# Projection stage of a hybrid decoder layer: new places for the weight sums, the row loads and the last group order, and outputs stored from ScalarE's queue

## The reference

```python
h = rms_norm(x, g_mix)                 # 2048 x 1024
proj = h @ w_in                        # 1024 x 7168, columns in 14 blocks of 512:
# q, k, v of three attention groups (9), the S5 input u (1), gate_a and gate_b (4)
q = head_rms_norm(q, q_gain) * HEAD_DIM ** -0.5     # norm over each head's 64
k = head_rms_norm(k, k_gain)
# gates: sigmoid(gate_a), sigmoid(gate_b)
```

## Time and profile before

| | us |
|---|---|
| three runs, median (lowest, highest) | 4801.2 (4799.83, 4801.86) |
| the profiled execution | 4802.6 |
| its span, first to last instruction | 4801.0 |
| its mean granted clock | 0.978 of full |

### The profile page before, as it was taken

How to read it: one execution, slowest core, us unless ns; L and a number is a source line. 1 busy time by engine, 2 the same in 40 slices (tenths; PEclk the granted TensorE clock), 3 DMA queues, 4 the chain that set the end, 5 groups by cost and what they waited for, 6 DMA issues and landing times.

```text
span 4801.0 us, 76663 instructions
## 1 busy us (share of the span) xinstructions
PE 4579.8 (95%) x25756; PEld 4000.1 (83%) x25756; DVE 3153.2 (66%) x6216; ACT 2181.2 (45%) x3608; POOL 928.7 (19%) x911
## 2 busy tenths in 40 slices
PE   7989899999889999999799999999999999999998
PEld 6767688777679987788699999999988888999997
DVE  6646674666456678555555556666667777778887
ACT  4444353444336673133233334344445555556665
POOL 1433200244212101222111111111121111111121
PEclk9999999999999999999899999999999999999999
DMA  6887665555654445543445555656566566677777
GB/s 205 278 301 239 235 202 169 156 164 176 185 191 141 135 164 183 186 135 135 169 159 172 189 182 189 206 179 216 180 222 222 208 232 242 236 245 269 279 262 256
DMA packets 341070, 971.18 MB, mean 202 GB/s; under 512 B 46057, under 2 KB 77588, under 8 KB 303317
## 3 DMA queue, kind: packets, MB, share of 16 engines
q1 hardware_dynamic: 307704, 862.90, 51.2%
q0 software_dynamic: 28304, 88.03, 7.9%
q10 hardware_dynamic: 4829, 17.31, 1.0%
HBM read 772.82 MB, written 200.58 MB: 203 GB/s over the span
## 4 chain that ended last, share of the span: by engine, by line
PE 50%; DVE 1%; ACT 0%; issue 0%; DVEq 0%; POOL 0%; DMA 0%; ACTq 0%; SPq 0%; POOLq 0%
PE ex_d L2794 14%; PE ex_g L2761 11%; PE ex_g L2763 9%; PE ex_g L2757 7%; PE ex_d L2757 4%; PE ex_d L2788 3%; PE ex_d L2763 2%; PE ex_g L2738 1%; PE ex_d L2738 0%; DVE ex_x L2956 0%; PE ex_d L2769 0%; DVEq L2565 0%; ACT ex_wgh L2841 0%; DVE ex_y L3030 0%; ACT ex_x L2854 0%
## 5 line engine op out<-in xcount | busy, mean ns | idle before, releaser
L2763 PE MATMUL ex_g<-ex_x,ex_wgl 128*128 128x256 f32 (+12 forms) x3456 | 981.1, 284 | 0.0
L2761 PE MATMUL ex_g<-ex_x,ex_wgh 128*128 128x288 f32 (+5 forms) x3584 | 757.7, 303 | 3.7 <-DVE ex_x L2956 3.7
L2763 PEld LDWEIGHTS ex_g<-ex_x,ex_wgl 128*128 128x128 f32 x3456 | 653.0, 189 | 3.9
L2938 DVE TENSOR_TENSOR ex_wgl<-ex_wg,ex_wgh 128x2048 fp32r<-128x2048 f32 x274 | 626.6, 2287 | 41.4 <-ACT ex_wgh L2841 41.3
L2841 ACT ACTIVATE ex_wgh<-ex_wg 128x2048 fp32r<-128x2048 f32 x274 | 523.8, 1912 | 284.0 <-PE ex_g L2763 275.7
L2761 PEld LDWEIGHTS ex_g<-ex_x,ex_wgh 128*128 128x128 f32 x3584 | 594.2, 188 | 12.8 <-DVE ex_x L2956 3.9
L2757 PE MATMUL ex_g<-ex_x,ex_wgh 128*128 128x512 f32 (+6 forms) x1664 | 529.5, 376 | 1.0 <-DVE ex_t L2968 1.0
L878 DVE TENSOR_TENSOR prj_wl<-prj_raw,prj_wh 128x512 fp32r<-128x512 f32 x396 | 314.5, 806 | 294.0 <-ACT prj_wh L756 293.3
L703 PE MATMUL prj_p<-prj_wh,prj_ah 128*128 128x512 f32 x1136 | 459.1, 404 | 44.9 <-DVE prj_wl L878 42.8
L703 PE MATMUL prj_p<-prj_wh,prj_al 128*128 128x512 f32 x1136 | 450.4, 396 | 0.0
L703 PE MATMUL prj_p<-prj_wl,prj_ah 128*128 128x512 f32 x1136 | 450.0, 396 | 0.0
(11 more groups left out here) (449 smaller groups left out, 9391.4 us busy)
## 6 DMA issues: line engine op xcount, KB each, us to landing
ex_wg<-in_w_gu SPq DMA_DIRECT2D x276, 1024.0 KB, 5.1
ex_wd<-in_w_down SPq DMA_DIRECT2D x276, 512.0 KB, 5.7
prj_raw<-sums_d SPq DMA_DIRECT2D x208, 256.0 KB, 3.1
prj_raw<-in_w_in SPq DMA_DIRECT2D x188, 256.0 KB, 3.0
qkv_d<-prj_o SPq DMA_DIRECT2D x144, 256.0 KB, 3.4
wo_spare<-qkv_d SPq DMA_DIRECT2D x40, 768.0 KB, 4.3
prj_wt<-in_w_in SPq DMA_DIRECT2D x56, 512.0 KB, 5.4
sums_d<-prj_wt SPq DMA_DIRECT2D x28, 1024.0 KB, 5.1
```

Source lines behind the costliest of these rows:

```text
L2761: pe.matmul(out[:, 0:size], h[:, k, j, :], x[:, k, 0:size], start=(k == 0 and x is xh), stop=False)
L2763: last = pe.matmul(out[:, 0:size], l[:, k, j, :], xh[:, k, 0:size], start=False, stop=(k == KD - 1))
L2938: tt(flat(wgl[z][:, :, :, :]), flat(wg[r][:, :, :, :]), flat(wgh[z][:, :, :, :]).bitcast(F32), ALU.subtract).then_inc(wgl_ready, 1)
```

## The change

The weight sums of pairs 1 to 6 are placed seven steps apart from step 4 on (before, all 28 in 5.78 steps each from step 8 on); those of pair 0 run at steps 226 to 247, and wait until the row blocks have left `wt`. Half 1 takes its pairs in the order 1, 4, 5, 0, 6, 2, 3 (before 0, 1, 4, 5, 6, 2, 3). Row tiles are loaded at `LOAD_AT` and normalised at `NORM_AT`, ahead of `TILE_AT`. `store` moves from SP to ScalarE, to the end of its step, behind the splits. The padding transfers are issued one every seven steps from 94 on, and VectorE makes three small groups a step in place of five.

```diff
-    for half, order in ((0, (0, 1, 2, 3, 4, 5, 6)), (1, (0, 1, 4, 5, 6, 2, 3))):
+    for half, order in ((0, (0, 1, 2, 3, 4, 5, 6)), (1, (1, 4, 5, 0, 6, 2, 3))):
...
+    LOAD_AT = {1: 3, 2: 4, 3: 5, 5: 6, 10: 7}
+    NORM_AT = {1: 2, 2: 3, 6: 4, 7: 5, 9: 6, 13: 7}
     TILE_AT = {1: 2, 2: 3, 9: 4, 11: 5, 13: 6, 15: 7}
     PAIR_AT = (42, 53, 64, 75)
-    SUM_AT = [8 + 156 * k // 27 for k in range(NQ * KH)]
+    LATER = KH * (NQ - 1)
+    SUM_AT = [4 + 7 * k for k in range(LATER)] + [226 + 7 * k for k in range(KH)]
...
+    PADS_AT = range(ZERO + 6, TABLES, 7)
...
-                        if half == 0:
+                        if half == 0 or q == 0:
                             sp.wait_ge(sum_out, 16 * SUMS.index((q, kk)) + 16)
...
-                    if k:
+                    if k == LATER:
+                        sp.wait_ge(turned, NB1)
+                    elif k:
                         sp.wait_ge(sum_out, 16 * k)
...
-                    if g == ZERO + 4:
-                        sp.wait_ge(zeroed, 1)
-                        for dst in pads:
-                            sp.dma_start(dst, xt[2][:, :]).then_inc(pads_out, 16)
+                    if g in PADS_AT[:len(pads)]:
+                        if g == PADS_AT[0]:
+                            sp.wait_ge(zeroed, 1)
+                        sp.dma_start(pads[PADS_AT.index(g)], xt[2][:, :]).then_inc(pads_out, 16)
+                    if g == PADS_AT[len(pads)]:
                         for dst, src in fills:
...
+                def store(e):
+                    g, kind, (_, where), half, upper, j = outs[e]
+                    if kind == Q:
+                        act.wait_ge(q_done, q_no[e] + 1)
+                    elif e in g_no:
+                        act.wait_ge(gated, g_no[e] + 1)
...
+                    act.dma_start(dst, ot[e % OR][:, :]).then_inc(o_out[e % OR], 16)
+
+                def store_at(e):
+                    g, kind = outs[e][:2]
+                    return g + (4 if kind == Q else 3 if e in g_no else 2)
...
-                for g in range(NSTEP + 3):
+                left = list(range(len(outs)))
+                for g in range(NSTEP + 4):
+                    if g in NORM_AT:
+                        square(NORM_AT[g])
+                        root(NORM_AT[g])
                     if g in TILE_AT:
                         b = TILE_AT[g]
-                        square(b)
-                        root(b)
                         high(2 * b)
                         high(2 * b + 1)
...
                         for s in splits_at(g):
                             split(s)
+                    while left and store_at(left[0]) <= g:
+                        store(left.pop(0))
...
+                    if g in NORM_AT:
+                        mean(NORM_AT[g])
+                        normalise(NORM_AT[g])
...
                     if MAPS <= g < TABLES:
-                        some(making_maps, 5)
+                        some(making_maps, 3)
```

More of the change, by code:

```diff
@@ L503, in load_block @@
                         sp.wait_ge(comb_out, stored[NJ])
-                        sp.wait_ge(sum_out, 16 * len(SUMS))
+                        sp.wait_ge(sum_out, 16 * LATER)
                     elif i >= NB0 + 4:
@@ L507, in load_block @@
                     sp.dma_start(dst, comb_d[j, o]).then_inc(sem, 16)
[L509 to L531, removed]
                 def load_maps():
@@ L575, in _ @@
                 loaded = KH + 1
-                left = list(range(len(outs)))
                 for g in range(NSTEP):
[L578 to L581, removed]
+                    if g in LOAD_AT:
+                        load_x(LOAD_AT[g])
                     ahead = min(NS, (g // NJ + 1) * KH + RAW + (0, 0, 1, 2)[g % NJ])
@@ L623, in _ @@
                 sp.wait_ge(pads_out, 16 * (len(pads) + len(fills)))
-                for e in left:
-                    store(e)
                 for z in range(2):
@@ L794, in head_squares @@
                         act.activation(sq[:, :], ot[e % OR][:, :], ACT.Square).then_inc(sq_ready, 1)
+                def store(e):
[4 more added lines that the diff above has]
+                        act.wait_ge(gated, g_no[e] + 1)
+                    elif g in act_post:
+                        act.wait_ge(act_done, act_post[g])
+                    else:
+                        act.wait_ge(dve_done, dve_post[g])
+                    t = 2 * NJ * half + NJ * upper + j
+                    if kind == GATE:
+                        c = 2 * half + upper
+                        dst = gate_d[:, where * NJ + j, c * CH:(c + 1) * CH]
+                    elif where is None:
+                        dst = u_d[t * P:(t + 1) * P, :]
+                    else:
+                        dst = qkv_d[where[0], t * P:(t + 1) * P, where[1], :]
+                    act.dma_start(dst, ot[e % OR][:, :]).then_inc(o_out[e % OR], 16)
+                def store_at(e):
+                    g, kind = outs[e][:2]
+                    return g + (4 if kind == Q else 3 if e in g_no else 2)
                 def head_roots(g):
@@ L1138, in _ @@
                 for g in range(NSTEP + 3):
+                    if g in NORM_AT:
+                        mean(NORM_AT[g])
+                        normalise(NORM_AT[g])
                     if g in TILE_AT:
                         b = TILE_AT[g]
-                        mean(b)
-                        normalise(b)
                         low(2 * b)
```

## The result

The changed kernel takes 4742.5 us (median of four runs, 4737.0 to 4743.5), the kernel before 4800.5 beside it (4793.0 to 4801.9): a ratio of 0.988, 95% interval 0.9863 to 0.9897. That is 58 us less, against 67 forecast (4734, range 4706 to 4768). The profiled execution took 4742.1 with a span of 4740.4; the projection's last matmul ends at 1213.9 us in place of 1274.7, 60.8 earlier, and the profiled executions differ by 60.5, so all of it came from the projection.

What follows compares the result with a forecast made beforehand. TensorE bounds the kernel, stalled in the projection by late weight slices queued behind SP's waits at sums. Gains 41 + 17 + 8 + 1 + 0 = 67 us gave 4734 us, range 4706 to 4768.

Steps and rivals of the forecast that it cites:

- The sum cycle: Weight sums' load, subtractions and store: 18.2 us with issues, too long for 15.7 us, just fitting seven steps, 19.0 us.
- Steps 32 to 115: Projection stretch with 58.5 us excess: queue waits go, DMA share 0.92 leaves 17; gain 41, bounds 36 and 58.
- Steps 116 to 171: Two q/k groups, excess 31.5 us: the stores' move decides, 14 kept; gain 17, bounds 3 and 22.
- The landing L: Time a q/k output store takes to land after ScalarE's issue; stores set VectorE's write period only from 6.1 us.
- Fewer small vector operations a step: VectorE's small groups in the projection's steps: gain 0, bounds 0 and 2 us.
- ScalarE's issues: 224 store issues of 0.34 us on ScalarE during the projection, delaying next to nothing: taken as 0.
- Rows ahead: First 17 steps: earlier row tile loads and norms remove PE's waits for tiles; gain 8 us, bounds 3 and 9.
- Half 1: Last four sums at steps 226 to 247 and the new pair order: gain 1 us, bounds -6 and +8.
- slower: Rival: ScalarE's late-landing stores close a loop with VectorE's writes in q/k groups; plus 43 us, 4844; chance 0.05.
- nothing: Rival: DMA sets the projection's pace, so fewer SP waits only move bytes; about 4797 us; chance 0.04.
- the waits only change place: Rival: sums' latency grows as DMA fills, SP stands again, q/k writes wait on stores; 4768 us; chance 0.16.
- all stalls go: Rival: all first-half stalls vanish, as DMA can run full and store landings are short; 4706 us; chance 0.13.

## Why the prediction was right, step by step
- *The sum cycle.* Right. 15.7 us didn't hold it: in the kernel before the loads of sums were 19.2 us apart in the mean of 22 gaps, with the dense sums put back 18.4, near the 18.2 that the prediction added up; and in the three kernels with dense sums steps 32 to 87 keep 29.1 to 30.6 us, in those with seven steps 15.6 to 23.3. The loads are now 20.7 us apart in the mean (58.1 at the second, 514.4 at the last of 22 gaps), not 19, which is seven steps at the pace that these steps had. It fits less well than the prediction had it: SP still waits 73 us at both lines, 30.8 of them at the first, where under 20 was said.
- *Steps 32 to 115: 41 forecast, 40.4 measured (287.8 to 247.4), the reason for the rest wrong.* That 17 us would stay, since DMA would be full at 0.92, came out in size alone, by luck: the stretch moved 73.1 MB, not 76.5, the share stayed at 0.85, and 11 MB more raised the stretch by 6 us. A share near 0.84 with PE still stalled was the prediction's own sign of being wrong; it was met, and it was this step that was wrong. What keeps the rest is open: 14.6 of the 18.5 us stand in products' first steps, behind VectorE's low halves, and most of the others in steps 37 and 38, where VectorE's write of an output is late.
- *Steps 116 to 171: 17 forecast, 16.7 measured, but not by its path.* The prediction said that the move of the stores decides here. Either change alone takes the excess: sums alone leave 5.4, stores alone 12.1, of 32.0. The full change keeps 15.4, of which 11.8 stand in steps 116 to 143; the next point has a likely reason. The landing L, where the danger was seen, is 3.6 us in these steps (median of the stores), within the 3 to 4 named beside the sum and far from 6.1; the loop doesn't close, though the 21 us named with it didn't come either. VectorE's writes in one group answer to the earlier trace rows, at 4.3 us a write:
```profile
516.02 0.69 DVE L895 TENSOR_TENSOR prj_o<-prj_p,prj_ua 128x512 f32<-128x512 f32 x1
...
519.83 0.69 DVE L895 TENSOR_TENSOR prj_o<-prj_p,prj_ua 128x512 f32<-128x512 f32 x1 [0.88 <-DMA qkv_d<-prj_o]
...
529.02 0.69 DVE L895 TENSOR_TENSOR prj_o<-prj_p,prj_ua 128x512 f32<-128x512 f32 x1
```
Of the four writes (another is at 523.93) only the second waited for a landing, 0.88 us where 5.16 had stood.
- *Fewer small vector operations a step: 0 forecast, never run alone.* Three groups a step in place of five last to step 124, where five end in step 112. In the first line below, the changed kernel, where step 116 begins at 368.5 us, some 20 us of this work fall in the first q/k group, in which VectorE is busiest; in the second, sums and order alone, all of it ends before that group (from 395.6):
```profile
L960 DVE TENSOR_SCALAR prj_x<-prj_x x10: 165/167/169, 376.6 to 398.0; 128x16 f32<-128x16 f32 x10
```
```profile
L957 DVE TENSOR_SCALAR prj_x<-prj_x x10: 160/167/169, 371.4 to 387.2; 128x16 f32<-128x16 f32 x10
```
All kernels with three groups have 7.4 to 13.4 us of excess in steps 116 to 143, sums and order alone has 1.5. Neither the stores, the row loads nor the padding, each put back alone, takes it away (9.9, 11.2, 7.4). Against that stand the 19.3 of steps 88 to 115 with five groups and the burst, where three and the burst have 7.7. What this part is worth in all, no run shows.
- *ScalarE's issues: 0.* Right: 0.33 us each, and twice the kernel without them was the same.
- *Rows ahead: 8 forecast, 6.9 measured in the window.* The waits for tiles 4, 5 and 7 are gone (7.2 us before). But the experiment gives only 1.7 us of it in the median, inside the noise. With the dense sums, the first at step 8, the first 17 steps have 14.3 us of excess, 3.0 less than the changed kernel: the sum at step 4, beside the tiles' loads, seems to take some of this gain.
- *Half 1: a gain of 1 forecast, a loss of about 2.5 measured.* The term that had the wrong sign, though inside its bounds of -6 and +8. Steps 200 to 283 lost 5.6: two q/k groups now stand there in place of one, and the last sums under one of them (1.7 less with these at step 207); steps 284 to 395 gained 3.1. The large transfer stayed, as said, and costs about 8 in both kernels, which the forecast hadn't priced.
- *Padding.* Not a term of its own in the sum; put back alone it costs 8 us.
- *The rule that issuing from several engines saves only issue time* (the Trainium skill, "DMA: Bandwidth & Descriptors", Issuing engines are not separate DMA queues): for the store move inside the changed kernel the runs agree, 0 within 3 us. On the kernel before they differ, and the measurement decides: it brought 12 us, since SP stood at waits with stores behind it in its list.
- The rivals: *slower* and *nothing* are disproved; *the waits only change place* by SP's waits, 73 us in place of 148, and by the share of 0.95 at 6 us; *all stalls go* by the 18.5 us left in steps 32 to 115.

What a part is worth depends on the others. The sums bring 41.5 us alone and 15 on top of the rest; the stores 12.4 alone and nothing on top; rows, padding and small groups together 15.9 beside the new sums (4756.1 to 4740.2), though rows and padding put back singly cost only 1.7 and 8. A reading that fits, though no run separates it: a wait of SP has to meet a slice or a store that is due, and any edit that empties the queue or shortens the wait removes the same stall.

## What to carry to other kernels
Lay an in-order queue's periodic work out by the length of its whole cycle (load, compute, store, landing), not by what spreads it evenly: one period too short, and the engine that issues stands at each round (148 us here), with everything behind it late. Before fearing that the memory is full, add traffic and look; and look for single large transfers ahead of small urgent ones, since cutting one in pieces was worth about 8 us, as much as spreading the padding. And work moved off a crowded stretch lands in another: look what that one does.

## What the runs showed of the hardware
ScalarE's queue took 224 stores beside SP's loads with an issue of 0.33 us. In steps 116 to 171 they landed in 3.6 us (median) at a share of 0.75, where SP's took 5.6 at 0.71 in the kernel before; in steps 32 to 115, at 0.85 and 0.84, it was 5.2 against 6.0. The changed kernel with the stores back on SP's queue is the cleaner pair: 5.3 and 5.8. In the long stretch the slices pay for it: they land in 6.0 us beside ScalarE's stores, in 4.9 with the stores on SP's queue, which may be why the move brings nothing. A split of VectorE (L884) takes 0.69 us in the mean (266 of them) and 1.09 where a GpSimd operation overlaps it (130), 1.6 times as long; the prediction had allowed for twice. And a DMA share of 0.95 at 332 GB/s lengthened 250 us of matmuls by no more than 6: the slices have three steps, 8.2 us, to land, and their median was 6.4.
